# Splitting the last multiply of a decoder block between VectorE and GpSimd

## The chip, the cores and the metric

The kernel runs on 1 core of one Trainium2 chip. The metric is the device time of one execution in microseconds (us), the median of several runs. Engines are called PE (TensorE), DVE (VectorE), ACT (ScalarE), POOL (GpSimd) and SP (SyncE); SP and ACT issue the DMAs that this case speaks of.

## The reference

One decoder block over 256 tokens of 2048 channels: two token mixers (Mamba-2 and S5), a gated merge, a gated MLP with a causal convolution, and a final RMSNorm. Only the last line matters here:

```
h = h + conv_glu_ffn(hn, w_up[i], conv_ffn_w[i], conv_ffn_b[i], w_down[i])
return rmsnorm(h, norm_final_w)     # h * rsqrt(mean(h*h over channels) + EPS) * w
```

## The kernel before

Data lies channel-major: 128 channels on the partitions and 256 tokens along the free axis, so the residual `h` and the weighed output `vn` are 16 tiles of 128x256 fp32 (128 KB each, 2.10 MB in all). Weights come in units of 128x1024 that ACT and DVE split into a high and a low part before PE multiplies them. That stream fills the program up to the last weight matmuls (L1989), some 10 us before its end.

The end of the program does the final RMSNorm. DVE multiplies each tile of `h` by its channel's weight as soon as the tile is complete (`weigh_out`, L1579, for tiles 0 to 13 during the last matmuls; `late_adds`, L1599, for tiles 14 and 15). ACT squares the tiles, POOL adds the squares into `sqacc` (L646, L649, L652), and PE sums them over the channels by matmuls against a column of ones (L2025, L2028) into `SUM_T`. ACT takes the square root (L1091), after a table load that it asks for early (L1089). DVE takes the reciprocal (L1744). That gives one number per token, with the tokens on the partitions. PE turns it into a row that is the same on all 128 partitions, by two transposes of a broadcast column, one for each 128 tokens (L2033), into `ROOT_T` in PSUM bank 6, and announces it with `row_ready`.

Then DVE multiplies `vn` in place by that row, read from PSUM (L1749), in nine pieces named in `PIECES`: two single tiles, then seven pairs of tiles. After each piece it counts up `v_ready`. SP waits for the pieces 0, 2, 4, 6, 8 and issues the DMA of each to the output (L418); ACT does so for the pieces 1, 3, 5, 7 (L1094). Both then wait until `out_done` has counted all of them, and the program ends. POOL has nothing to do after L652. Its waits and instructions run in program order on each engine, so an instruction behind a wait starts only when the wait is over.

Two more names: `rs` is a 128x256 SBUF tile that holds the roots of earlier norms and is free at the end, and `LAST`, in PSUM bank 7, holds the last partial sums of tile 15 until DVE has added them (L1597).

Of the kernel before, what the change touches and what calls it, by code (L numbers as in the profile page):

```python
# [25 lines left out]
ALU, ACTF = mybir.AluOpType, mybir.ActivationFunctionType  # L26
ds = bass.ds

P = 128
L = 256  # L30
# [7 lines left out]
KT = D_MODEL // P  # L38
# [28 lines left out]
    _at += _w  # L67
N_PARM = _at

PIECES = [(0, 1), (1, 2)] + [(k, k + 2) for k in range(2, KT, 2)]  # L70

N_UP = PHASES["up"][0] // 2

# [35 lines left out]
def build_program(nc, a, out):  # L109
    ctx = ExitStack()  # L110
    with ctx:
# [4 lines left out]
        def at(name, shape, dt, off):  # L116
            size = 4 * math.prod(shape[1:])
            assert off + size <= room, (name, off, size, room)
            return nc.alloc_sbuf_tensor_at(name, shape, dt, offset=base + off)
# [8 lines left out]
        vn = at("vn", [P, KT, L], F32, 80 * K)  # L128
# [9 lines left out]
        h = at("h", [P, KT, L], F32, 168 * K)  # L138
# [52 lines left out]
        rs = at("rs", [P, L], F32, C + 8832)  # L191
        sq = at("sq", [P, 2, L], F32, 185 * K)
        sqacc = at("sqacc", [P, 2, L], F32, 187 * K)
        rcol = at("rcol", [P, 2, 1], F32, 184 * K)
        ident_end = at("ident_end", [P, P], F32, 184 * K + 64)
# [7 lines left out]
        psum = ctx.enter_context(nc.psum_tensor("psum", [P, 8, 512], F32))  # L203
# [5 lines left out]
        DTS = psum[:, 4, 0:L]  # L209
        SUM_T, ROOT_T = psum[:, 4:6, 0:1], psum[:, 6, 0:L]  # L210
        LAST = psum[:, 7, 0:L]
        DTT = psum[:, 5:7, ML:ML + HEADS]

        def sem(name):
# [4 lines left out]
        parm_in, s5_in, h_in, out_done, scr_w = map(sem, ("parm_in", "s5_in", "h_in", "out_done", "scr_w"))  # L219
# [31 lines left out]
        ns_free, late_sum, late_h = map(sem, ("ns_free", "late_sum", "late_h"))  # L251
        ident_ready, sum_t_ready, root_ready, inv_ready, row_ready = map(
            sem, ("ident_ready", "sum_t_ready", "root_ready", "inv_ready", "row_ready"))
        ysum_ready, yz_ready, ysq_ready, yns_ready, yrs_ready, yv_ready, yhi_ready, ylo_ready = map(
            sem, ("ysum_ready", "yz_ready", "ysq_ready", "yns_ready", "yrs_ready", "yv_ready", "yhi_ready", "ylo_ready"))

# [12 lines left out]
        def col(name, n):  # L269

            return parm[:, ds(n + PARM[name], 1)]
# [24 lines left out]
        def _(sp):  # L296
# [51 lines left out]
            for name in list(PHASES)[1:]:  # L348
# [26 lines left out]
                if name in TOKEN_MAJOR:  # L375
                    w = a["w_" + name].rearrange("(c g q) p (h n) -> c q h p g n", g=2, q=quads, h=2)
                    for j in range(groups * quads):
                        n, c, q, half = UNIT0[name] + j, j // (2 * quads), j % (2 * quads) // 2, j % 2
# [5 lines left out]
                if name in MIXED:  # L384
                    w = a["w_" + name].rearrange("(c g q) p (h n) -> c q h p g n", g=2, q=quads, h=2)
                    for j in range(groups * quads):
                        n, c, q, half = UNIT0[name] + j, j // (2 * quads), j % (2 * quads) // 2, j % 2
# [12 lines left out]
                with sp.Fori(0, groups // per) as i:  # L400
                    for j in range(per * quads):
                        n = UNIT0[name] + j
# [6 lines left out]
                        if name == "u" and 2 <= j < 10:  # L409
                            if j == 2:  # L410
                                sp.wait_ge(const_ready, 3)
                            r, g = (j - 2) // 2, j % 2
                            row = 32 * r + 16 * g
                            sp.dma_start(bz[row:row + 16, :, 64 * g:64 * g + 64],
                                         a["s5_b"][2 * r + g]).then_inc(b0_in, 16)
            for c, (k0, k1) in list(enumerate(PIECES))[::2]:
                sp.wait_ge(v_ready, 4 + c + 1)
                sp.dma_start(out[:, k0:k1, :], vn[:, k0:k1, :]).then_inc(out_done, 16)  # L418
            sp.wait_ge(out_done, 16 * len(PIECES))


        @block.gpsimd
        def _(pool):
            step = Tally(pool, pool_step)
# [225 lines left out]
            pool.wait_ge(sqacc_ready, 18)  # L650
            pool.wait_ge(sq_ready, 16)
            nc.gpsimd.tensor_tensor(sqacc[:, 0, :], sqacc[:, 0, :], sq[:, 0, :], ALU.add).then_inc(sqacc_ready, 1)  # L652


        @block.scalar
        def _(act):
            step = Tally(act, act_step)
            fn = nc.scalar.activation
# [51 lines left out]
            def group_hsum(name, i, r):  # L710
                _, per, quads, u0, g0 = phase(name)
                take_hsum(g0 + r, u0 + (r + 1) * quads, i * per, i * (per * quads))
# [51 lines left out]
            def group_tap(name, i, r):  # L764

                _, per, quads, u0, g0 = phase(name)
                if name == "u" or name == "zx" and r % 2 == 0:
                    return
                act.wait_ge(sum_ready, i * per + (g0 + r + 1))
                act.nop(nofuse=True)  # L770
                for t in range(2):
                    if name == "zx":
                        to, q = zx[:, ds(i * 4 + (r - 1 + t), 1), 1, :], i * 4 + (r - 1 + t)
                    else:
                        to, q = bc[:, ds(i * 4 + r, 1), t, :], i * 8 + (24 + 2 * r + t)
                    ins = fn(to.rearrange("p o n -> p (o n)"), cpad[:, t, 3:3 + L], ACTF.Identity,
                             scale=col("conv_a_w", q * 4 + 3), bias=col("conv_a_b", q))
                ins.then_inc(tap_ready, 1)

            def group_silu(name, i, r):  # L780

                _, per, quads, u0, g0 = phase(name)
                if name == "u":
                    return
                if name == "zx" and r % 2 == 0:
                    act.wait_ge(sum_ready, i * per + (g0 + r + 1))
                    to = zx[:, ds(i * 4 + r, 2), 0, :]
                    fn(to, to, ACTF.Silu).then_inc(z_done, 1)
                elif name == "zx":
                    act.wait_ge(conv_done, i * 2 + (r // 2 + 1))  # L790
                    act.nop(nofuse=True)
                    to = zx[:, ds(i * 4 + (r - 1), 2), 1, :]
                    fn(to, to, ACTF.Silu).then_inc(xbc_done, 1)
                else:
                    act.wait_ge(conv_done, i * per + (12 + r + 1))
                    to = bc[:, ds(i * 4 + r, 1), :, :].rearrange("p o c n -> p (o c) n")
                    fn(to, to, ACTF.Silu).then_inc(xbc_done, 1)
# [195 lines left out]
            for s in range(32):  # L993
# [3 lines left out]
                c, j = s // 8 - 1, s % 8  # L997
# [68 lines left out]
            for s in range(88):  # L1066
# [4 lines left out]
                c, j = s // 22 - 1, s % 22  # L1071
# [17 lines left out]
                    fn(tsum[:, 0, 0:1], ones[:, 0:1], ACTF.Sqrt)  # L1089
            act.wait_ge(sum_t_ready, 1)  # L1090
            fn(rcol[:, :, :], SUM_T, ACTF.Sqrt, bias=EPS, scale=1.0 / D_MODEL).then_inc(root_ready, 1)  # L1091
            for c, (k0, k1) in list(enumerate(PIECES))[1::2]:
                act.wait_ge(v_ready, 4 + c + 1)
                act.dma_start(out[:, k0:k1, :], vn[:, k0:k1, :]).then_inc(out_done, 16)  # L1094
            act.wait_ge(out_done, 16 * len(PIECES))


        @block.vector
        def _(dve):
            step = Tally(dve, dve_step)  # L1100
            V = nc.vector
# [247 lines left out]
            def mixer_turn(name, i, blk, prev):  # L1349

                _, per, quads, u0, g0 = phase(name)
                start = prev[0] == "u"
                for r in range(per):
# [52 lines left out]
            def gate_turn(i, prev, first_scan=False, next_scan=True):  # L1406
# [19 lines left out]
                def tokens():  # L1426
# [3 lines left out]
                    if prev is None:  # L1430
                        step.done(V.tensor_copy(dtt[:, :, :], DTT))
                    for k in range(2):
# [139 lines left out]
            def weigh_out(g):  # L1572

                if g < 6:
                    dve.wait_ge(down_added, g // 2 + 1)
                else:
                    dve.wait_ge(sum_ready, GROUP0["down"] + (g - 5))
                for k in (2 * g, 2 * g + 1):
                    step.begun(V.tensor_scalar(vn[:, k, :], h[:, k, :], col("norm_final", k), None, ALU.mult))  # L1579

            def weighed_h_lo(g):
                dve.wait_ge(hwhi_ready, g + 1)
# [3 lines left out]
            def late_adds(t):  # L1586
# [6 lines left out]
                else:  # L1593
                    mul(h[:, k, :], sums(g, 1)[:, t, :], h[:, k, :], ALU.add)
                    dve.wait_ge(late_sum, 3)
                    for half in (slice(0, P), slice(P, L)):
                        V.tensor_tensor(h[:, k, half], LAST[:, half], h[:, k, half], ALU.add).then_inc(late_h, 1)  # L1597
                dve.wait_ge(late_h, 2 * t + 1)
# [34 lines left out]
            for s in range(32):  # L1633
# [5 lines left out]
                c, j = s // 8 - 1, s % 8  # L1639
# [85 lines left out]
            for s in range(88):  # L1725
# [4 lines left out]
                c, j = s // 22 - 1, s % 22  # L1730
# [15 lines left out]
            dve.wait_ge(row_ready, 1)  # L1746
            for k0, k1 in PIECES:
                row = ROOT_T.rearrange("p (o n) -> p o n", o=1).to_broadcast([P, k1 - k0, L])
# [4 lines left out]
        def _(pe):  # L1753
# [84 lines left out]
            for k in range(KT):  # L1838
                ins = mm(DTS[64 * (k % 2):64 * (k % 2) + 64], wdt[:, k, :], xin[:, k, :], start=k < 2, stop=k >= KT - 2)
# [60 lines left out]
            def gate_turn(i, prev):  # L1900
# [25 lines left out]
                if prev is None:  # L1926
                    pe.wait_ge(dt_row, 1)
                    for k in range(2):
                        rows = slice(64 * k, 64 * k + HEADS)
                        nc.tensor.transpose(DTT[:, k, :], rs[rows, 0:P], ident[rows, rows])  # L1930
                for k in range(2):
# [34 lines left out]
            def late_tile(t):  # L1966
# [17 lines left out]
                if t == 1:  # L1984
                    for q in (quads - 2, quads - 1):
                        s = (UNIT0["down"] + (2 * per - 1) * quads + q) % RING
                        for k in range(4):
                            x, w = ff[:, 4 * q + k + KT, 0:L], slice(k * L + P, k * L + 2 * P)
                            ins = mm(LAST, whi[:, s, w], x, start=q == quads - 2 and k == 0,  # L1989
                                     stop=q == quads - 1 and k == 3)  # L1990
# [35 lines left out]
            for t in range(2):  # L2026
                pe.wait_ge(sq_ready, 17 + t)
                ins = mm(SUM_T[:, t, :], sq[:, 1, t * P:t * P + P], ones[:, 0:1], start=False, stop=True)  # L2028
            ins.then_inc(sum_t_ready, 1)
            pe.wait_ge(ident_ready, 1)  # L2030
            pe.wait_ge(inv_ready, 1)
            for t in range(2):
                ins = nc.tensor.transpose(ROOT_T[:, t * P:t * P + P], rcol[:, t, :].to_broadcast([P, P]),  # L2033
                                          ident_end[:, :])
            ins.then_inc(row_ready, 1)

    return nc

# [71 lines left out]
```

## Time and profile before

| | |
|---|---|
| runs | median 1680.54 us of 3 (1680.04 to 1681.38) |
| profiled execution | 1680.3 us, of which 1678.6 us are the span |
| PE busy | 1667.1 us, 99% of the span |
| last matmul with a weight ends | 1668.2 us |
| DVE's first output multiply | 1670.70 us |
| last output DMA issued | 1675.66 us |

The span runs from the first to the last instruction of the core; 1.7 us of the execution lie around it. Times of the trace are counted from the span's start. Each engine's instructions are listed by source line. A DMA has two times: when the engine's queue issues it, and when it lands, which is when its semaphore is counted up.

### The profile page before, as it was taken

Reading aid. Unit: us, or ns where it says so; the run is one execution under the profiler, and the core shown is the slowest. Engines: PE = TensorE matmul, PEld = TensorE weight load, DVE = VectorE, ACT = ScalarE, POOL = GpSimd, SP = SyncE. Lnnn points to the kernel's source line nnn. Section 1 sums busy time; section 2 is a strip of 40 time slices with the busy share of each in tenths; the row PEclk is TensorE's granted clock in tenths of the full one; section 3 lists DMA queues with packets and bytes.
Section 4 is the critical chain, followed back from the end, with each engine's and each line's share of the span. In section 5 each row is a group of like instructions: output and inputs, shape, how many; then the busy total and the mean of one; then the engine's idle time right before and its main releaser. Section 6 shows DMA issues by size and latency. Waiting matters only on the chain.

```text
span 1678.6 us, 24422 instructions
## 1 busy us (share of the span) xinstructions
PE 1667.1 (99%) x8340; PEld 1395.1 (83%) x8340; DVE 1320.3 (79%) x1685; ACT 962.7 (57%) x1271; POOL 216.4 (13%) x310
## 2 busy tenths in 40 slices
PE   9999999999999999999999999999999999999997
PEld 8888888888788888888888888888888888888886
DVE  7999999999998986545775868888878888845555
ACT  7676676766666667444557755444444444454553
POOL 7843342221000000000000200000000000000001
PEclk9999999999999999999999999999999999999999
DMA  7666766666666566656786577777777777666653
GB/s 254 213 197 199 204 206 200 193 188 190 194 217 231 191 219 189 199 191 201 239 254 232 174 233 241 243 241 244 242 244 241 245 232 248 225 194 195 191 189 123
DMA packets 174569, 358.49 MB, mean 214 GB/s; under 512 B 16880, under 2 KB 39584, under 8 KB 174368
## 3 DMA queue, kind: packets, MB, share of 16 engines
q1 hardware_dynamic: 162528, 338.26, 62.5%
q0 software_dynamic: 11248, 18.37, 4.6%
q8 instruction: 41, 0.67, 0.2%
q10 hardware_dynamic: 720, 0.93, 0.2%
q14 instruction: 32, 0.26, 0.0%
HBM read 335.41 MB, written 15.80 MB: 209 GB/s over the span
## 4 chain that ended last, share of the span: by engine, by line
PE 73%; DVE 2%; issue 0%; ACT 0%; DVEq 0%
PE psum L1822 22%; PE psum L1823 22%; PE psum L1824 22%; PE psum L1783 3%; PE psum L1785 2%; PE psum L1908 1%; DVE wlo L1107 0%; PE psum L1909 0%; DVE vn L1749 0%; PE psum L1933 0%; DVE bc L1303 0%; PE psum L1829 0%; PE psum L1924 0%; DVE dec L1416 0%; PE psum L1982 0%; PE psum L1979 0%
## 5 line engine op out<-in xcount | busy, mean ns | idle before, releaser
L1107 DVE TENSOR_TENSOR wlo<-raw,whi 128x1024 fp32r<-128x1024 f32 x580 | 709.6, 1230 | 321.3 <-ACT whi L666 314.0
L666 ACT ACTIVATE whi<-raw 128x1024 fp32r<-128x1024 f32 x580 | 611.9, 1058 | 577.1 <-PE psum L1824 455.1
L1783 PE MATMUL psum<-act,whi 128*128 128x512 f32 x1088 | 342.5, 396 | 0.0
L1822 PE MATMUL psum<-whi,nw 128*128 128x512 f32 x704 | 274.1, 389 | 0.0
L1824 PE MATMUL psum<-whi,nw 128*128 128x512 f32 x704 | 273.9, 389 | 0.0
L1823 PE MATMUL psum<-wlo,nw 128*128 128x512 f32 x704 | 273.9, 389 | 0.0
L1785 PEld LDWEIGHTS psum<-act,wlo 128*128 128x128 f32 x1088 | 204.4, 188 | 48.3
L1785 PE MATMUL psum<-act,wlo 128*128 128x256 f32 x1088 | 213.7, 278 | 0.0
L1783 PEld LDWEIGHTS psum<-act,whi 128*128 128x128 f32 x1088 | 165.6, 189 | 3.3 <-issue 2.8
L1824 PEld LDWEIGHTS psum<-whi,nw 128*128 128x128 f32 x704 | 132.1, 188 | 27.6
L1822 PEld LDWEIGHTS psum<-whi,nw 128*128 128x128 f32 x704 | 132.1, 188 | 27.3
L1823 PEld LDWEIGHTS psum<-wlo,nw 128*128 128x128 f32 x704 | 132.1, 188 | 27.3
L1822 PE MATMUL psum<-whi,act 128*128 128x512 f32 x352 | 138.8, 394 | 0.8 <-DVE wlo L1107 0.8
L1824 PE MATMUL psum<-whi,act 128*128 128x512 f32 x352 | 137.1, 390 | 0.0
L1823 PE MATMUL psum<-wlo,act 128*128 128x512 f32 x352 | 137.1, 389 | 0.0
L1822 PE MATMUL psum<-whi,ff 128*128 128x512 f32 x264 | 102.7, 389 | 0.0
L1823 PE MATMUL psum<-wlo,ff 128*128 128x512 f32 x264 | 102.7, 389 | 0.0
L1824 PE MATMUL psum<-whi,ff 128*128 128x512 f32 x264 | 102.7, 389 | 0.0
L1822 PEld LDWEIGHTS psum<-whi,act 128*128 128x128 f32 x352 | 66.1, 188 | 16.2 <-DVE wlo L1107 1.6
L1824 PEld LDWEIGHTS psum<-whi,act 128*128 128x128 f32 x352 | 66.1, 188 | 13.9
L1823 PEld LDWEIGHTS psum<-wlo,act 128*128 128x128 f32 x352 | 66.1, 188 | 13.1
L1303 DVE SCALAR_TENSOR_TENSOR fsum<-cpad,parm,fsum 128x256 f32<-128x256 f32 x176 | 76.9, 478 | 0.0
(251 smaller groups left out, 2300.3 us busy)
## 6 DMA issues: line engine op xcount, KB each, us to landing
raw<-in_w_up SPq DMA_DIRECT2D x176, 512.0 KB, 4.9
raw<-in_w_zx SPq DMA_DIRECT2D x96, 512.0 KB, 3.7
raw<-in_w_down SPq DMA_DIRECT2D x88, 512.0 KB, 3.8
raw<-in_w_gate SPq DMA_DIRECT2D x64, 512.0 KB, 5.6
raw<-in_w_proj SPq DMA_DIRECT2D x48, 512.0 KB, 4.4
raw<-in_w_bc SPq DMA_DIRECT2D x32, 512.0 KB, 3.7
raw<-in_w_glu SPq DMA_DIRECT2D x32, 512.0 KB, 4.4
raw<-in_w_out SPq DMA_DIRECT2D x32, 512.0 KB, 4.8
```

What stands on the lines that cost most here:

```text
L666: fn(whi[:, s, :], raw[:, s, :], ACTF.Copy).then_inc(hi_ready, 1)
L1107: V.tensor_tensor(wlo[:, s, :], raw[:, s, :], whi[:, s, :], ALU.subtract).then_inc(lo_ready, 1)
L1303: ins = V.scalar_tensor_tensor(to[t], src, col(w, q * taps + k), to[t], ALU.mult, ALU.add)
L1783: mm(psum[:, b + t, :], whi[:, s, cols(t)], x, start=first, stop=False)
L1785: ins = mm(psum[:, b + t, L:2 * L], wlo[:, s, cols(t)], x[:, 0:L], start=False, stop=last)
L1822: mm(banks[:, t, :], x_hi, high[:, k], start=j == 0 and k == 0, stop=False)
L1823: mm(banks[:, t, :], x_hi, low[:, k], start=False, stop=False)
L1824: ins = mm(banks[:, t, :], x_lo, high[:, k], start=False, stop=last and k == 1)
L1908: mm(y, xtok[:, 0, x], dec[half][:, k, 0:L], start=True, stop=False)
```

## The change

GpSimd multiplies tiles 0 to 3, in two pairs, and VectorE the other twelve, in two single tiles and five pairs. GpSimd reads the row from SBUF: PE writes the row a second time, into PSUM bank 7 (`ROOT_AGAIN`, where `LAST` was), ACT waits for it, copies it into `rs`, and counts up `row_copied`. GpSimd also waits until the four tiles have been weighed (`weighed_first`). ACT issues the output DMAs of GpSimd's pieces among its own: DVE's pieces 1 and 3, GpSimd's first, DVE's piece 5, GpSimd's second. SP issues DVE's pieces 0, 2, 4 and 6. There are nine output DMAs before and after.

```
-PIECES = [(0, 1), (1, 2)] + [(k, k + 2) for k in range(2, KT, 2)]
+POOL_PIECES = [(0, 2), (2, 4)]
+PIECES = [(4, 5), (5, 6)] + [(k, k + 2) for k in range(6, KT, 2)]
...
+        ROOT_AGAIN = psum[:, 7, 0:L]
...
+        weighed_first, row_copied, pool_done = map(sem, ("weighed_first", "row_copied", "pool_done"))
...
-            sp.wait_ge(out_done, 16 * len(PIECES))
+            sp.wait_ge(out_done, 16 * (len(PIECES) + len(POOL_PIECES)))
...
+            pool.wait_ge(weighed_first, 4)
+            pool.wait_ge(row_copied, 1)
+            for k0, k1 in POOL_PIECES:
+                row = rs[:, :].rearrange("p (o n) -> p o n", o=1).to_broadcast([P, k1 - k0, L])
+                nc.gpsimd.tensor_tensor(vn[:, k0:k1, :], vn[:, k0:k1, :], row, ALU.mult).then_inc(pool_done, 1)
...
+            act.wait_ge(row_ready, 2)
+            fn(rs[:, :], ROOT_AGAIN, ACTF.Copy).then_inc(row_copied, 1)
             for c, (k0, k1) in list(enumerate(PIECES))[1::2]:
                 act.wait_ge(v_ready, 4 + c + 1)
                 act.dma_start(out[:, k0:k1, :], vn[:, k0:k1, :]).then_inc(out_done, 16)
-            act.wait_ge(out_done, 16 * len(PIECES))
+                if c > 1:
+                    k0, k1 = POOL_PIECES[c // 2 - 1]
+                    act.wait_ge(pool_done, c // 2)
+                    act.dma_start(out[:, k0:k1, :], vn[:, k0:k1, :]).then_inc(out_done, 16)
+            act.wait_ge(out_done, 16 * (len(PIECES) + len(POOL_PIECES)))
...
-                    step.begun(V.tensor_scalar(vn[:, k, :], h[:, k, :], col("norm_final", k), None, ALU.mult))
+                    ins = V.tensor_scalar(vn[:, k, :], h[:, k, :], col("norm_final", k), None, ALU.mult)
+                    if k < 4:
+                        ins.then_inc(weighed_first, 1)
+                    else:
+                        step.begun(ins)
...
-            for t in range(2):
-                ins = nc.tensor.transpose(ROOT_T[:, t * P:t * P + P], rcol[:, t, :].to_broadcast([P, P]),
-                                          ident_end[:, :])
-            ins.then_inc(row_ready, 1)
+            for to in (ROOT_T, ROOT_AGAIN):
+                for t in range(2):
+                    ins = nc.tensor.transpose(to[:, t * P:t * P + P], rcol[:, t, :].to_broadcast([P, P]),
+                                              ident_end[:, :])
+                ins.then_inc(row_ready, 1)
```

## Rows read from the trace of the kernel before

**Rows 1.** The page: the span, then busy time of two engines.

```profile
span 1678.6 us, 24422 instructions
PE 1667.1 (99%) x8340; PEld 1395.1 (83%) x8340; DVE 1320.3 (79%) x1685; ACT 962.7 (57%) x1271; POOL 216.4 (13%) x310
```

**Rows 2.** The chain that ended last, from 1670 us: start us, us, what.

```profile
1670.18 0.42 PE psum L2033 x2
...
1670.70 0.42 DVE vn L1749
...
1671.45 4.18 DVE vn L1749 x7
```

**Rows 3.** Timeline: start us, us, engine, line, instruction, count, idle before and releaser.

```profile
1670.18 0.40 PE L2033 MATMUL psum<-ident_end,rcol 128*128 128x128 f32 x2 [0.55 <-DVE rcol L1744]
1671.04 1.01 DVE L1749 TENSOR_TENSOR vn<-vn,psum 128x256 f32<-128x256 f32 x2
1674.95 0.68 DVE L1749 TENSOR_TENSOR vn<-vn,psum 128x512 f32<-128x512 f32 x1
```

**Rows 4.** Timeline of the queues that issue output DMAs, first, third, last.

```profile
1671.14 0.34 SPq L418 DMA_DIRECT2D out<-vn  x1
1671.48 0.34 ACTq L1094 DMA_DIRECT2D out<-vn  x1
1672.07 0.34 SPq L418 DMA_DIRECT2D out<-vn  x1
1675.66 0.33 SPq L418 DMA_DIRECT2D out<-vn  x1
```

**Rows 5.** DMA view, 1671 to 1679 us in 40 slices of 0.2 us.

```profile
DMA  0000089983999999999999999999999997000000
GB/s 0 0 0 0 26 287 348 353 277 133 399 369 358 410 358 379 410 358 379 410 359 379 420 348 379 420 359 348 420 379 359 399 389 277 0 0 0 0 0 0
DMA packets 1296, 2.10 MB, mean 262 GB/s; under 512 B 144, under 2 KB 400, under 8 KB 1296
```

**Rows 6.** DMA view, single issues at 1672.07 and 1675.66: KB, us to landing.

```profile
out<-vn SPq DMA_DIRECT2D x1, 256.0 KB, 2.1
out<-vn SPq DMA_DIRECT2D x1, 256.0 KB, 2.6
```

**Rows 7.** Windows: engines' busy us, then PE clock, DMA share, GB/s.

```profile
1673.00:1674.00 1.00, 0.00 (x0) 0.00 (x0) 1.00 (x3) 0.00 (x0) 0.00 (x0) 0.50 1.03 379
1674.00:1675.00 1.00, 0.00 (x0) 0.00 (x0) 1.00 (x3) 0.00 (x0) 0.00 (x0) 0.50 1.04 387
1675.00:1676.00 1.00, 0.00 (x0) 0.00 (x0) 0.63 (x2) 0.00 (x0) 0.00 (x0) 0.50 1.02 377
1676.00:1677.00 1.00, 0.00 (x0) 0.00 (x0) 0.00 (x0) 0.00 (x0) 0.00 (x0) 0.50 1.03 385
```

**Rows 8.** ScalarE, groups by shape: busy us, mean ns; then its table load's timeline.

```profile
L677 ACT ACTIVATE rs<-psum 128x256 f32<-128x256 f32 x10 | 3.9, 386 | 0.1
1666.81 1.28 ACT L1089 ACT_TABLE_LOAD   x1
1668.66 0.51 ACT L1087 ACTIVATE sq<-h 128x128 f32<-128x128 f32 x2 [0.36 <-DVE h L1597]
```

**Rows 9.** GpSimd's 128x512 additions, all 15: duration ns min/median/max.

```profile
L646 POOL TENSOR_TENSOR sqacc<-sqacc,sq x15: 1290/1682/2178, 906.9 to 1643.1; 128x512 f32<-128x512 f32 x15
```

**Rows 10.** Timeline of GpSimd and VectorE where they overlap near the end.

```profile
1639.32 1.76 POOL L646 TENSOR_TENSOR sqacc<-sqacc,sq 128x512 f32<-128x512 f32 x1 [0.80 <-ACT sq L977]
1639.90 1.73 DVE L1124 TENSOR_TENSOR h<-h,hsum 128x512 f32<-128x512 f32 x1
1641.66 0.69 DVE L1622 TENSOR_TENSOR h<-psum,h 128x512 f32<-128x512 f32 x1
1666.38 0.42 ACT L1087 ACTIVATE sq<-h 128x256 f32<-128x256 f32 x1 [8.20 <-DVE h L1592]
1666.93 0.74 POOL L652 TENSOR_TENSOR sqacc<-sqacc,sq 128x256 f32<-128x256 f32 x1 [20.86 <-ACT sq L1087]
1667.31 0.42 DVE L1124 TENSOR_TENSOR h<-psum,h 128x256 f32<-128x256 f32 x1 [0.64 <-PE psum L1982]
```

## The prediction

> **What bounds the kernel now.** I read the page first: PE is busy 99% of 1678.6 us [rows 1], and nothing in the diff touches the part where PE works. What the change can move lies between PE's row and the last instruction, so I went to the end of the chain of waits. It runs through the two transposes, then through DVE's multiplies one after another [rows 2]. Read alone, the chain says that DVE sets the end and that work taken from it is time saved. It stops at DVE's last multiply, though, and the span goes on for 3 us more, so the third view is the DMAs.
>
> The timeline gives DVE's pace: the second single starts at 1671.04 and the first pair ends at 1672.05, so with a duration of 0.68 us the first pair starts at 1671.37. The last starts at 1674.95 [rows 3]. Six steps in 3.58 us are 0.597 us for a pair of 262,144 bytes, or 439 GB/s. The DMAs' pace is in the windows: 379, 387, 377 and 385 GB/s in four full microseconds, at a busy share of 1.02 to 1.04 [rows 7], mean 382. One pair takes 0.686 us. So the DMAs are slower than DVE, and the slices show no gap between 1673.0 and 1677.7 [rows 5]. The landing times say the same: 2.1 us for the first pair, 2.6 us for the last [rows 6]; the difference of 0.5 us is the queue built up in front of it.
>
> So I lay the DMAs' schedule beside the issues. A single issued at 1671.14 [rows 4] brings data from about 1672.0 (a fifth slice with 26 GB/s, a sixth with 287 [rows 5]), 0.88 us later. The third piece, a pair, is issued at 1672.07 [rows 4], so its data flow from 1672.95. That fits the hole in the slices, 277 and 133 GB/s, just ahead of it [rows 5]. From there seven pairs at 0.686 us give 1677.75, and the slices stop at 1677.8. To keep this stream unbroken, the pairs must be issued by 1672.07, 1672.76, 1673.44, 1674.13, 1674.82, 1675.50 and 1676.19. DVE's pace gives 1672.07, 1672.67, and so on to 1675.66 [rows 4]. Only the first is tight; the last is 0.53 us early. The end is set by the moment of the third piece and by the bytes.
>
> **The change part by part.** The sum is made against the profiled execution: 1680.3 us, of which 1678.6 are the span. It lies 0.24 us under the median of the three runs.
>
> DVE loses two pairs, 2 x 0.597 = 1.19 us. Its last multiply ends at 1674.44 instead of 1675.63. Its first three pieces are of the same shapes as before, now tiles 4, 5 and 6-7, and end at the same times. So the two singles and the third piece are issued as before, and nothing shortens the part ahead of 1672.95.
>
> PE writes ROOT_T first and announces it, so DVE starts at 1670.70 as before. The second pair of transposes takes at most the 0.40 us of the first [rows 3], to 1670.98, when PE has nothing else to do. DVE reads another bank meanwhile.
>
> ACT's copy of 128x256 from PSUM costs 0.39 us, by the logarithm of the same shape [rows 8]. With 0.03 us for the wait it runs from 1671.01 to 1671.40. Behind it on ACT stands the DMA of piece 1, issued at 1671.48 before [rows 4]. The cover is thus only 0.08 us. If it is missed by 0.1 or 0.2 us, the second single's data come that much later, and the hole of 1672.6 to 1673.0 takes it up: its two slices fell to 277 and 133 of 382 [rows 5], 0.18 us of idle DMA. I take 0. A table load ahead of the copy would cost 1.28 us [rows 8]. The square right behind the root's load needed none [rows 8], though no row has a copy there. I take none. With one, piece 1 would be issued at 1672.76 and the DMAs would stand idle between the first single, done by 1672.34, and 1672.95, so one single's 0.34 us (half of 0.686) moves behind the pairs: bounds 0 and +0.34 us.
>
> GpSimd starts about 0.13 us after its releaser, as L652 did behind ACT's square (1666.38 + 0.42 to 1666.93 [rows 10]): 1671.53. No row shows a multiply of a pair by a repeated row. The nearest are its 15 additions of the same 128x512 size, 1.29 to 2.18 us, median 1.68 [rows 9]. At 1.3 us each the pieces are ready at 1672.83 and 1674.13, at 2.18 us at 1673.7 and 1675.9. I take 1.3, because the longer ones overlapped a DVE instruction with two SBUF inputs. Near the end DVE's addition of that kind took 1.73 us beside a GpSimd one, against 0.69 us for the same size with an input in PSUM and GpSimd idle [rows 10]. L1749 reads its row from PSUM, and the one row of such an instruction started beside a GpSimd addition is 0.42 us [rows 10], no longer than the 0.42 us of L1749 itself. So DVE keeps its pace.
>
> The rule behind that is in the Trainium skill, SBUF — State Buffer, section "Who interferes with whom": a DVE instruction with at most one SBUF input, outside the two-port modes, does not contend with GpSimd, while one with two SBUF inputs blocks against a GpSimd instruction that reads SBUF. By that rule the sum keeps its zero here; the case in which it did not hold is the second rival.
>
> The pairs are then issued at about 1672.07 (DVE), 1672.67 (DVE), 1672.86 (GpSimd), 1673.27, 1673.87 (DVE), 1674.16 (GpSimd) and 1674.47 (DVE). An issue takes 0.34 us of its queue [rows 4], and ACT's five are further apart than that where they matter. Each moment is at or ahead of the schedule above. Even additions of 2.18 us would give the last at 1675.9, 0.3 us ahead of 1676.19. ACT waits for GpSimd ahead of DVE's piece 5, but SP's pieces keep the DMAs fed. The count, the bytes and the completions of the output DMAs are the same. The four weighings of tiles 0 to 3 only count up another semaphore, long before.
>
> Sum: DVE -1.19 us, all of it in front of a queue that is not emptied earlier: 0 on the path. PE 0, ACT 0, GpSimd 0. The execution stays at 1680.3 us, its median at 1680.5 us.
>
> **The rivals.** First, the DMAs aren't at a limit and follow DVE. Then the end moves with DVE's last piece, by -1.19 us, to 1679.3 us. For it: the chain of waits ends in DVE, and some slices reach 420 GB/s [rows 5]. Against it: landing grows from 2.1 to 2.6 us, and the microsecond from 1676, after DVE has stopped, runs at the same 385 GB/s as those before [rows 7]. A milder form is that deeper queues get the 420 GB/s throughout: seven pairs in 4.37 us instead of 4.80, -0.4 us, 1680.1 us.
>
> The Trainium skill, DMA: Bandwidth & Descriptors, section "Specifications", gives two ceilings, 435 GB/s for the fabric and about 358 for one core's share of HBM. The 382 GB/s here lie between. By the first the seven pairs would be an estimated 4.2 us, by the second 5.1 us; the measured rate is above the lower ceiling, so the trace decides.
>
> Second, on the other side: DVE and GpSimd exclude each other although the row is in PSUM. Then from 1671.53 on, DVE's remaining 2.9 us and GpSimd's 2.6 us stand in line. The last pair is ready at 1677.05 instead of 1675.63 and lands 2.1 us after its issue (the unloaded value [rows 6]), at 1679.2 instead of 1678.26: +0.9 us, 1681.4 us. It decides from the point where the last pair is issued after 1676.19, which needs 2.3 us for each of GpSimd's two. For it: 1.73 us for DVE [rows 10]. Against it: the row of 0.42 us, which only began beside GpSimd for its last 0.36 us.
>
> Third, the copy needs a table load and delays piece 1: +0.3 us, 1680.8 us. With a GpSimd at 2.18 us as well, the last piece is issued at 1677.2 and this grows to about +1.0 us.
>
> **How the numbers follow.** No change 0.77; the DMAs a little faster 0.06; DVE's pace sets the end 0.05; exclusion 0.06; table load or a delayed issue 0.05; something outside these 0.01. 0.2% is 3.4 us, about what a measurement of this kernel can tell from no change. None of the mechanisms reaches it: they span -1.2 to +1.0 us, so the chance of the same is 0.97, and 0.01 and 0.02 are left for what I don't see, with a little more for slower since the change adds waits. The range is the likeliest case with the spread of the median, about 0.5 us by the three runs, widened to the milder case below (1680.1 less 0.5) and to exclusion above: 1679.6 to 1681.4 us.
>
> **What would show it.** Right: DVE's seven instructions of L1749 end at about 1674.4; the output's DMA slices are full from 1673.0 to about 1677.75 as before; the last landing takes some 3.7 us instead of 2.6; GpSimd's two multiplies take about 1.3 us each from 1671.5, with DVE's at 0.68 us beside them; no table load at the copy. Wrong: slices that end at 1676.6; DVE's at well over 0.68 us; GpSimd's second ending after 1676.2; ACT's first issue later than 1671.6.

## The result, and the profile after

The changed kernel takes 1684.16 us (median of 14 runs, 1683.09 to 1686.14) against 1680.53 us before (14 runs): ratio 1.0021, 95% interval 1.0013 to 1.0028. That is 3.6 us slower where no change was forecast, and above the range of 1679.6 to 1681.4 us. The profiled execution's span went from 1678.6 to 1682.2 us.

The last timeline of the changed kernel, from the square root on, answers to [rows 3, 4, 10] (start us, us, engine, line, instruction, count, idle before and releaser):

```profile
1669.76 0.17 ACT L1099 ACTIVATE rcol<-psum 128x2 f32<-128x2 f32 x1 [0.50 <-PE psum L2046]
...
1670.27 0.62 PE L2052 MATMUL psum<-ident_end,rcol 128*128 128x128 f32 x4 [0.55 <-DVE rcol L1762]
1670.79 3.74 DVE L1767 TENSOR_TENSOR vn<-vn,psum 128x256 f32<-128x256 f32 x7 [0.66 <-PE psum L2052]
1670.93 0.38 ACT L1101 ACTIVATE rs<-psum 128x256 f32<-128x256 f32 x1 [1.00 <-PE psum L2052]
1671.23 3.65 SPq L421 DMA_DIRECT2D out<-vn  x4
1671.46 2.50 POOL L660 TENSOR_TENSOR vn<-vn,rs 128x512 f32<-128x512 f32 x2 [3.69 <-ACT rs L1101]
1671.57 1.53 ACTq L1104 DMA_DIRECT2D out<-vn  x2
1673.14 0.48 ACTq L1108 DMA_DIRECT2D out<-vn  x1
1673.96 0.34 ACTq L1104 DMA_DIRECT2D out<-vn  x1
1674.34 0.95 ACTq L1108 DMA_DIRECT2D out<-vn  x1
```

Nothing here is late. DVE's multiplies start 0.09 us later than before, as the whole program up to there does, and end at 1674.53. GpSimd's end at 1673.96. The DMA view from 1671 to 1679 us in slices of 0.2 us shows the same stream as [rows 5], with the same hole before the third piece and an end at about 1677.85 (1677.75 before):

```profile
GB/s 0 0 0 0 0 164 364 328 353 103 338 379 338 420 369 348 410 369 389 399 358 379 369 389 379 379 389 379 389 379 359 389 399 389 92 0 0 0 0 0
```

So the span goes on for 4.4 us after the last byte, against 0.8 us before. What fills it isn't in any busy row, since the instructions at the end of a block don't count as busy. They are listed under L111 (L112 after), in whose scope the block is closed. One of them is DRAIN, a row of its own for every engine; it can start while the engine's last instruction is still running, and its duration then holds the rest of that instruction too. First the kernel before (duration ns min/median/max, first and last start us):

```profile
L111 POOLq EVENT_SEMAPHORE  x2: 17/17/17, 1678.5 to 1678.5; - x2
L111 POOLq DRAIN  x1: 8822/8822/8822, 1666.9 to 1666.9; - x1
...
L111 SPq COMPARE_BRANCH  x1: 38/38/38, 1678.2 to 1678.2; - x1
L111 ACTq COMPARE_BRANCH  x1: 38/38/38, 1678.3 to 1678.3; - x1
L111 SPq DRAIN  x1: 7/7/7, 1678.4 to 1678.4; - x1
...
L111 SPq EVENT_SEMAPHORE  x1: 17/17/17, 1678.6 to 1678.6; - x1
```

And the changed kernel, the same view:

```profile
L112 POOLq EVENT_SEMAPHORE  x2: 17/17/17, 1682.1 to 1682.1; - x2
...
L112 POOLq DRAIN  x1: 10543/10543/10543, 1671.5 to 1671.5; - x1
L112 SPq COMPARE_BRANCH  x1: 38/38/38, 1678.3 to 1678.3; - x1
...
L112 SPq EVENT_SEMAPHORE  x1: 17/17/17, 1682.2 to 1682.2; - x1
```

SP leaves its wait on the output DMAs (COMPARE_BRANCH) at 1678.2 before and 1678.3 after: the outputs are written at the same time. Then every engine waits at the block's end, and the last to come is GpSimd. Its DRAIN begins when its last instructions have been issued and outlives them by a long time, so GpSimd does have something left to do after L652, though no busy row shows it. Before: 1666.93 + 8.82 = 1675.75, where L652 had ended at 1667.67 [rows 10], 8.08 us after it. After: 1671.46 + 10.54 = 1682.00, where the second multiply had ended at 1673.96, 8.04 us after it. Before, that lay 2.7 us ahead of the others' arrival. After, it comes 3.5 us behind.

### The profile page after: what moved, and what is told of

Its sections match the earlier page's. It is cut to its first block, busy times and chain, and to the rows that moved or that the text cites. A ratio compares the mean times of both kernels' runs of the same rounds, so it can differ in the third digit from the quotient of the medians.

```text
span 1682.2 us, 24428 instructions
## 1 busy us (share of the span) xinstructions
PE 1666.9 (99%) x8342; PEld 1394.5 (83%) x8342; DVE 1318.5 (78%) x1683; ACT 963.0 (57%) x1272; POOL 219.0 (13%) x312
## 3 DMA queue, kind: packets, MB, share of 16 engines
q10 hardware_dynamic: 864, 1.19, 0.2%
## 4 chain that ended last, share of the span: by engine, by line
PE 73%; DVE 2%; issue 0%; ACT 0%; DVEq 0%
PE psum L1840 22%; PE psum L1841 22%; PE psum L1842 22%; PE psum L1801 3%; PE psum L1803 2%; PE psum L1926 1%; DVE wlo L1121 0%; PE psum L1927 0%; PE psum L1951 0%; DVE bc L1317 0%; PE psum L1847 0%; DVE vn L1767 0%; PE psum L1942 0%; DVE dec L1430 0%; PE psum L2000 0%; PE psum L1997 0%
```

## The experiments

Theory A: GpSimd's DRAIN at the end of the block takes about 8.05 us from its last instruction on, whatever that was, and everything waits for it. Its rivals: the added transposes, copy and waits (B); GpSimd's writes or the barrier (the point at the block's end where every engine waits for the others) come back late in another way (C); the size of the multiplies (D). Two theories refine A: the 8.05 us count from the moment at which the DRAIN is reached with the engine idle (A2), and they are owed for GpSimd's DMAs and paid once (E). GpSimd issues 124 DMAs in this program, all long before the end. As the program up to the final norm varies by over 1 us from one execution to the next, I compare the profiles by the stretch from DVE's first output multiply to the span's end, which is read to 0.1 us: 7.9 us before (1670.70 to 1678.6), 11.4 us after (1670.79 to 1682.2).

Ratios are to runs of the kernel before that were taken together with each experiment. Their medians are 1680.71 us (22 runs) for `row_and_copy`, `after_no_drain`, `memset_late` and `wait_only`, 1680.49 us (27) for `one_piece`, `before_no_drain`, `drains_mid` and `four_singles`, and 1680.34 us (21) for the other three. The experiments' own medians are of 11 runs, of 5 for `memset_late`; `wait_only`, `drains_mid` and `three_drains` have one run each.

**Without GpSimd's multiplies** (`row_and_copy`). DVE multiplies all sixteen tiles; the second row and the copy stay.

```
-POOL_PIECES = [(0, 2), (2, 4)]
-PIECES = [(4, 5), (5, 6)] + [(k, k + 2) for k in range(6, KT, 2)]
+POOL_PIECES = []
+PIECES = [(0, 1), (1, 2)] + [(k, k + 2) for k in range(2, KT, 2)]
...
-            pool.wait_ge(weighed_first, 4)
-            pool.wait_ge(row_copied, 1)
...
```

Two conditions left out here are set so that ACT issues no DMA of GpSimd's and all weighings count up the semaphore of before.

> The change without GpSimd's two multiplies: TensorE writes the row twice, ScalarE copies it, VectorE multiplies all sixteen tiles in the nine pieces of before. Theory A (GpSimd's DRAIN at the end of the block ends 8.05 us after GpSimd's last instruction, and everything waits for it): GpSimd's last instruction is L652 again, its DRAIN ends at about 1675.7 us, hidden; the span is that of before, 1678.6 us, the median 1680.5. Rival B (the added transposes, the copy ahead of ScalarE's DMA issues or the extra waits cost the time): the span stays near 1682 us.

1680.30 us, ratio 1.0000 (0.9991 to 1.0009); the stretch is 7.95 us (1670.35 to 1678.3). GpSimd's DRAIN starts with L652 again and takes the 8.82 us of before. Rival B falls: PE's second pair of transposes and ACT's copy cost nothing.

**Without the DRAIN** (`after_no_drain`). The changed kernel, one argument different.

```
-        block = ctx.enter_context(nc.Block())
+        block = ctx.enter_context(nc.Block(no_gpsimd_drain=True))
```

> The changed kernel, with the block told to leave out GpSimd's DRAIN at its end. Theory A: the 3.6 us vanish, the span is 1678.5 to 1678.8 us as the output DMAs end it, the median 1680.5. Rival C (GpSimd itself, or its writes, come back late whatever waits for them, or the barrier takes its time elsewhere): the span stays near 1682 us, or the time returns outside the span and the execution stays at 1684 us.

1681.31 us, ratio 1.0001 (0.9992 to 1.0010); the stretch is 8.0 us (1670.57 to 1678.6). GpSimd still multiplies, from 1671.24 for 2.50 us, and the time is gone. It doesn't return outside the span either. Rival C falls. It also gives the change without its side effect: no loss, and no gain that the stretches show (8.0 against 7.9 us), though DVE's multiplies take 3.74 us instead of 4.93.

**One column, late** (`memset_late`) and **no instruction at all** (`wait_only`), both in the kernel before; the memset stands in `memset_late` alone:

```
             nc.gpsimd.tensor_tensor(sqacc[:, 0, :], sqacc[:, 0, :], sq[:, 0, :], ALU.add).then_inc(sqacc_ready, 1)
+            pool.wait_ge(v_ready, 4 + len(PIECES))
+            nc.gpsimd.memset(rs[:, 0:1], 0.0)
```

> The kernel before, with one GpSimd instruction more: a memset of one column of the dead tile rs, after VectorE's last output multiply (1675.65 us). It does next to no work and touches no output. Theory A: it ends at about 1676.1, the DRAIN at 1676.1 + 8.05 = 1684.2, the span is 1684.3 us (+5.7), the execution 1686.2. Rival D (the 3.6 us came from the size of GpSimd's two multiplies, 2.5 us of work and 0.5 MB written): a memset of one column costs under 1 us.

> The kernel before, with GpSimd waiting for VectorE's last output multiply (1675.65 us) at its end, and no instruction behind the wait but the DRAIN. Theory A as stated (8.05 us from the end of the last instruction, in the engine): the engine has long been idle, the DRAIN ends at 1675.8 or little later and the span is 1678.6 us. Theory A2 (8.05 us from the moment at which the DRAIN is reached and the engine is idle): the DRAIN ends at 1683.7, the span is 1683.9 us (+5.3).

`memset_late`: 1686.72 us, ratio 1.0035 (1.0022 to 1.0049), stretch 13.4 us (1670.38 to 1683.8). `wait_only`: 1686.45 us in its one run, stretch 13.4 us (1671.41 to 1684.8). GpSimd's DRAIN, first in `memset_late`, then in `wait_only`:

```profile
L111 POOLq DRAIN  x1: 8155/8155/8155, 1675.4 to 1675.4; - x1
```

```profile
L111 POOLq DRAIN  x1: 8030/8030/8030, 1676.5 to 1676.5; - x1
```

0.10 us of memset, or nothing, cost more than 0.5 MB of multiplies did (6.0 and 5.7 us against 3.6), since the DRAIN was reached later. Rival D falls. So does theory A as first stated: in `wait_only` the engine had been idle for 8 us when the DRAIN was reached, and it still took 8.03. What holds is A2: 8.03 us from the moment at which the DRAIN is reached and the engine is idle.

**One multiply** (`one_piece`). GpSimd takes tiles 0 and 1, DVE the other fourteen.

```
-POOL_PIECES = [(0, 2), (2, 4)]
-PIECES = [(4, 5), (5, 6)] + [(k, k + 2) for k in range(6, KT, 2)]
+POOL_PIECES = [(0, 2)]
+PIECES = [(2, 3), (3, 4)] + [(k, k + 2) for k in range(4, KT, 2)]
...
```

The waits and the order of ACT's DMAs are fitted to the one piece.

> The changed kernel with GpSimd multiplying one pair of tiles (0 and 1) instead of two, VectorE the other fourteen in the nine minus one pieces. Theory A2 (GpSimd's DRAIN at the block's end lasts about 8.05 us from the moment its last instruction is done, and all engines wait for it): the only multiply starts about 0.76 us after VectorE's first output multiply starts, as in the changed kernel (1671.46 less 1670.79 is 0.67), and ends 1.27 us later; the DRAIN's end is 1.25 us earlier than in the changed kernel, the span 2.3 to 2.4 us above before's, the execution about 1683.0 us. If instead the mere presence of GpSimd work at the end cost a fixed 3.6 us, the time would stay at 1684.2 us.

1682.97 us, ratio 1.0015 (1.0006 to 1.0024); the stretch is 10.2 us (1670.21 to 1680.4), between 7.9 and 11.4 and 1.2 us under the changed kernel for one multiply of 1.27 us less. The multiply ends at 1672.15, the DRAIN at 1680.2:

```profile
L112 POOLq DRAIN  x1: 9348/9348/9348, 1670.9 to 1670.9; - x1
```

The loss is not a fixed fee for using GpSimd: it grows with the moment at which GpSimd is done.

**The kernel before without the DRAIN** (`before_no_drain`), the same argument.

> The kernel before with GpSimd's DRAIN at the block's end left out. Theory A2: it ended at about 1675.7 us, 2.7 us ahead of the end of the output DMAs, so it was hidden: no change, span 1678.6, median 1680.5 to 1680.8. If the DRAIN held something else back (the barrier, the DMAs' engines), leaving it out gains up to a microsecond.

1680.30 us, ratio 0.9998 (0.9989 to 1.0007), stretch 8.0 us. The DRAIN was hidden, as its place in the trace says.

**Two DRAINs in idle time** (`drains_mid`), in the kernel before:

```
                 nc.gpsimd.memset(sqacc[:, :, :], 0.0).then_inc(sqacc_ready, 1)
+                if n == 1:
+                    nc.gpsimd.drain()
+                    nc.gpsimd.drain()
```

> The kernel before with two DRAINs more on GpSimd, back to back, at about 1451 us, where GpSimd is idle for some 65 us. Theory A2 with a fixed price: each of the two takes about 8 us. Rival E (the 8 us are for what GpSimd's DMAs left behind, and one DRAIN settles it): the first takes 8 us and the second far less, and the DRAIN at the end is short too. Either way they lie in idle time and the span stays 1678.6 us.

The rows of the first, the second, and the one at the end:

```profile
L644 POOLq DRAIN  x1: 8592/8592/8592, 1450.6 to 1450.6; - x1
...
L645 POOLq DRAIN  x1: 47/47/47, 1459.3 to 1459.3; - x1
...
L111 POOLq DRAIN  x1: 832/832/832, 1666.7 to 1666.7; - x1
```

Rival E is right. The first takes 8.59 us, of which 0.53 are the memset in front of it; the second takes 0.05 us; the one at the end 0.83 us, of which 0.74 are L652. The run took 1680.07 us, with a span of 1678.4. The 8 us are a debt that the first DRAIN pays, and the nine additions behind it (seven 128x512 ones and the last two) don't renew it.

**The changed kernel with one early DRAIN** (`after_early_drain`).

```
                 nc.gpsimd.memset(sqacc[:, :, :], 0.0).then_inc(sqacc_ready, 1)
+                if n == 1:
+                    nc.gpsimd.drain()
```

> The changed kernel with one DRAIN more on GpSimd, at about 1451 us, where it is idle for 65 us. By the run with two DRAINs there (8.59 us the first, 0.05 the second, 0.83 the one at the end, of which 0.74 are the addition in front of it), a DRAIN settles something that GpSimd's instructions before it left behind, once. Then the early one takes about 8 us in idle time, the one at the end ends 0.1 us after GpSimd's second multiply, at 1674.1, and the span is 1678.6 us again: 3.6 us less than the changed kernel, median 1680.5. Theory A2 with a price at every DRAIN, which that run speaks against, would leave 1684.2.

1680.91 us, ratio 1.0001 (0.9992 to 1.0010), stretch 7.9 us (1671.56 to 1679.5). The early DRAIN takes 8.59 us at 1451.7 and hides. The last is done with the multiplies:

```profile
L112 POOLq DRAIN  x1: 2560/2560/2560, 1672.2 to 1672.2; - x1
```

The cure needs no option of the block, only an instruction at a moment when GpSimd has nothing to do.

**What the debt is for** (`three_drains`): one DRAIN after 108 of GpSimd's 124 DMAs, one after 15 more, just ahead of the load of `h` (the expectation says 16).

```
             pool.wait_ge(y5_ready, 8)
+            nc.gpsimd.drain()
             load_decay(0, 1)
...
             pool.wait_ge(m_read, 128)
+            nc.gpsimd.drain()
             pool.dma_start(h[:, :, :], a["x"]).then_inc(h_in, 16)
```

> The kernel before with two DRAINs more on GpSimd, one after about 108 of its 124 DMAs (8 MB, about 9,000 packets), one just ahead of the last (after 16 of them, 9 MB, about 2,100 packets), so that only the load of h (1 DMA, 2.1 MB, 144 packets) stands ahead of the one at the end. If the 8.05 us are so much for each DMA (65 ns), the three cost about 7.0, 1.0 and 0.1 us beyond what the engine still has to do; for each packet 6.4, 1.5 and 0.1; for each byte 3.2, 3.9 and 0.9; if it is a fixed price after any DMA, 8 us each, and the end is as before (8.8 us with L652). The first may be longer, as a load is still under way.

```profile
L621 POOLq DRAIN  x1: 8887/8887/8887, 441.0 to 441.0; - x1
...
L630 POOLq DRAIN  x1: 1280/1280/1280, 884.1 to 884.1; - x1
...
L111 POOLq DRAIN  x1: 926/926/926, 1676.4 to 1676.4; - x1
```

Packets, MB and share of what GpSimd's DMAs moved ahead of each, up to 441 us, from there to 884.5 us, and behind it:

```profile
q0 software_dynamic: 8944, 7.42, 10.5%
...
q0 software_dynamic: 2160, 8.85, 6.0%
...
q0 software_dynamic: 144, 2.10, 0.6%
```

Each DRAIN pays for what was added since the last. Between the first two GpSimd executes nothing but its 15 loads, and the second comes 267 us after the last of them was issued, so it is the DMAs that have a price, and not their being under way. Nor was one under way at the first, as the expectation feared: the last load, issued at 432.18, had landed after 5.1 us, by 438. A fixed price falls (8 us three times), and so do bytes (7.42 MB cost 8.84 us, 8.85 MB cost 1.23, and the load of `h`, 2.1 MB, 0.93 - 0.83 = 0.09 us). Between a price for each DMA and one for each packet it isn't settled: for each DMA 82, 82 and 94 ns here (8.84, 1.23 and 0.09 us, the 0.05 of an empty DRAIN taken off the first two) but 64 in `wait_only` (7.98 us for 124); for each packet, with 8,944, 2,160 and 144 of them, 0.99, 0.57 and 0.65 ns, and 0.71 in `wait_only`. The parts add up to 10.2 us, not 8.0, which neither explains. The run's time, 1689.79 us, is longer since the first DRAIN stood in the way of a load that work waits for: the load is issued at 450.48 instead of 441.49, and PE is busy for 4.87 of the 10 us from 450, where it was busy throughout.

**Four single tiles ahead** (`four_singles`, in the kernel before, and `early_drain_four`, in the changed kernel with the early DRAIN), a test of the prediction's other step:

```
-PIECES = [(0, 1), (1, 2)] + [(k, k + 2) for k in range(2, KT, 2)]
+PIECES = [(k, k + 1) for k in range(4)] + [(k, k + 2) for k in range(4, KT, 2)]
```

That is the edit in the kernel before; `early_drain_four` makes tiles 4 to 7 single and leaves four pairs to DVE.

> The kernel before with four single tiles and six pairs as pieces, instead of two and seven: a test of the prediction's other step, that the output DMAs and the moment of the third piece set the end. The third piece, a single, is ready 0.26 us earlier than the pair was, so the hole in the DMA slices after the second single (0.18 us) closes: from VectorE's first output multiply to the last landing 0.15 to 0.2 us less than before's 7.5 us. The median moves by less than can be told. If VectorE's pace set the end, its two more instructions (0.15 us of overhead in all at most) would make the same stretch no shorter.

> The same early DRAIN, and four single tiles ahead of VectorE's pairs: what both findings together give. The span is set by the output DMAs; the hole behind the second single closes, so from VectorE's first output multiply to the end of the waits on the DMAs 7.3 to 7.4 us instead of 7.5. Median 1680.3; not to be told from before by its time.

1679.99 us, ratio 0.9998 (0.9989 to 1.0007), and 1680.55 us, ratio 1.0003 (0.9994 to 1.0012). The DMA view of `four_singles`, in the same slices, whose DVE starts 0.38 us earlier than before's:

```profile
GB/s 0 0 0 287 348 333 353 323 333 343 282 379 389 348 410 379 358 410 359 389 410 348 379 410 359 359 430 379 359 410 369 256 0 0 0 0 0 0 0 0
DMA packets 1440, 2.10 MB, mean 262 GB/s; under 512 B 160, under 2 KB 672, under 8 KB 1440
```

The hole is gone, as expected, and the stretch is the same 7.9 us, which wasn't: the singles move at 323 to 353 GB/s where pairs move at 382, with 672 packets under 2 KB instead of 400 [rows 5]. At their mean of 339 the two more singles lose an estimated 0.09 us, and the slice of 282 GB/s behind them loses 0.05, together most of the hole's 0.18. `early_drain_four` missed its expectation in the same way: its waits on the DMAs end 7.5 us after DVE's first multiply, not 7.3 to 7.4, and its stretch of 7.8 us is within the reading of 7.9. No version here beats the kernel before.

## Why the prediction was wrong

The step that failed is the sum, "GpSimd 0". It followed GpSimd's work up to the moment at which its tiles are ready to be sent (1674.16 forecast, 1673.96 measured) and compared that with the DMAs' schedule. It asked nothing of what GpSimd still has to do after its last instruction. The deadline of 1676.19 us for the last pair was right for the DMAs. A second and far earlier one stood beside it: GpSimd must be done 8.05 us ahead of the moment at which the others reach the block's end. With that at 1678.4, GpSimd had to be done by 1670.35, before PE's row even exists (1670.6). As long as the DRAIN's 8 us were left to the end, no GpSimd work on the last row could be hidden, whatever its size. 1673.96 less 1670.35 is 3.6 us, the loss.

The price stood in the trace of before, in the row of 8822 ns under L111; no row of it was among those that the prediction rests on. It is not counted as busy, it isn't in the chain of waits, and its end at 1675.75 falls 0.12 us behind the end of DVE's last multiply (1675.63), so it looks like a wait for DVE. The sentence ahead of the prediction that GpSimd has nothing to do after L652 is wrong for the same reason. The statement that the mechanisms span -1.2 to +1.0 us was a statement on those that had been listed, and the 0.02 for slower was too small for a change that makes an idle engine the last to finish.

The rest, step by step:

- *The output DMAs set the end, DVE's 1.19 us are worth 0.* Right: with the DRAIN out of the way (`after_no_drain`, `after_early_drain`) the stretch is 8.0 and 7.9 us against 7.9. The last landing takes 3.8 us (forecast 3.7). The first rival, DVE's pace, falls with it, and so does its milder form: with deeper queues the slices from 1673.2 on still have a mean of 380 GB/s.
- *PE's second pair and ACT's copy hide.* Right, by `row_and_copy`. The copy ran from 1670.93, 0.38 us (0.39 forecast), ahead of piece 1's issue at 1671.57, with no table load: the third rival falls.
- *GpSimd's multiplies take 1.3 us and DVE keeps its pace.* Right. Duration ns min/median/max in the changed kernel:

```profile
L660 POOL TENSOR_TENSOR vn<-vn,rs x2: 1266/1268/1271, 1671.5 to 1672.7; 128x512 f32<-128x512 f32 x2
```

```profile
L1767 DVE TENSOR_TENSOR vn<-vn,psum x7: 414/678/679, 1670.8 to 1673.8; 128x512 f32<-128x512 f32 x5, 128x256 f32<-128x256 f32 x2
```

  DVE's pairs take 0.68 us beside GpSimd's, as alone [rows 3]. The second rival falls. The rule of the Trainium skill (SBUF — State Buffer, section "Who interferes with whom"), that a DVE instruction with at most one SBUF input, outside the two-port modes, doesn't contend with GpSimd, agrees with these rows.
- *The hole behind the second single costs 0.18 us.* Right as a reading; closing it with smaller pieces gained nothing that could be measured.

## What to carry to other kernels

Before giving an engine work near the end, look at what it does there between its last instruction and the barrier, DRAINs included: the engine's deadline is the barrier less that, not the moment at which its data are needed. On a GpSimd that had issued 124 DMAs that was 8 us here; a DRAIN placed in its idle time after the last of them reduced it to 0.1 us. And where an engine handed its results to a DMA stream that was already full, relieving that engine was worth nothing, however plainly the chain of waits named it.

## What the runs showed of the hardware

- GpSimd's DRAIN takes 8.03 us after 124 DMAs issued from it, 0.05 us right behind another DRAIN, 1.28 us after 15 more DMAs, and the engine's being idle beforehand doesn't shorten it. SP's and ACT's take 7 and 8 ns, though SP has issued several hundred DMAs; the traces list those under hardware_dynamic queues and GpSimd's under a software_dynamic one. Whether the price goes by DMA or by packet, and why the parts add up to more than the whole, stays open.
- A DMA issue on ACT's queue, 0.34 us as a rule [rows 4], took 0.48 and 0.95 us for GpSimd's two pieces, when more pieces were on their way than before (landing 3.8 instead of 2.6 us). It cost nothing here; why it takes longer wasn't tried.
- 128 KB output pieces go out at 323 to 353 GB/s in `four_singles`, 256 KB pieces at 382.
